# MLP down projection: the low parts of half of the ordinary weight loads are made by ScalarE and an accumulating GpSimd transfer instead of by VectorE

## The reference

```python
u = jax.nn.relu(rms_norm(h, mlp_norm_g) @ w_up)
h = h + (u * u) @ w_down
```

## Time and profile before

| | |
|---|---|
| time, median of 3 runs (lowest to highest) | 2503.59 us (2503.17 to 2504.42) |
| span of the profiled execution | 2504.0 us |
| TensorE busy | 2480.6 us (99%) |
| VectorE busy | 1753.6 us (70%) |
| ScalarE busy | 1257.8 us (50%) |
| GpSimd busy | 29.5 us (1%) |
| DMA queue of the loads | 463.53 MB, 55.2% of 16 engines |
| chain that ended last | PE 94%, issue 4%, DVE 2% |

### The profile page before, as it was taken

How to read it: one execution, slowest core, us unless ns; L and a number is a source line. 1 busy time by engine, 2 the same in 40 slices (tenths; PEclk the granted TensorE clock), 3 DMA queues, 4 the chain that set the end, 5 groups by cost and what they waited for, 6 DMA issues and landing times.

```text
span 2504.0 us, 38061 instructions
## 1 busy us (share of the span) xinstructions
PE 2480.6 (99%) x15416; PEld 2115.6 (84%) x15416; DVE 1753.6 (70%) x1978; ACT 1257.8 (50%) x1506; POOL 29.5 (1%) x26
## 2 busy tenths in 40 slices
PE   9999999999999999999999999999999999999998
PEld 7888888888888888888888888888888888888886
DVE  6656765668668677675777777775776666777777
ACT  7655344544444444445555555544654444444543
POOL 0000000000000000000000000000000000000000
PEclk9999999999999999999999999999999999999999
DMA  9454545546546546555545454556465565556553
GB/s 381 153 183 152 176 153 193 176 164 223 193 161 231 187 171 211 193 195 183 185 153 185 153 185 153 185 170 195 150 217 185 186 200 187 183 194 198 186 188 127
DMA packets 128239, 465.97 MB, mean 186 GB/s; under 512 B 14368, under 2 KB 14624, under 8 KB 127168
## 3 DMA queue, kind: packets, MB, share of 16 engines
q1 hardware_dynamic: 127920, 463.53, 55.2%
q10 hardware_dynamic: 144, 0.02, 0.0%
HBM read 461.39 MB, written 2.10 MB: 185 GB/s over the span
## 4 chain that ended last, share of the span: by engine, by line
PE 94%; issue 4%; DVE 2%; ACT 0%; DMA 0%; SPq 0%; DVEq 0%; POOL 0%; POOLq 0%
PE job L970 30%; PE job L982 16%; PE job L938 11%; PE job L940 11%; PE job L939 11%; PE job L957 2%; PE job L958 2%; PE job L959 2%; PE att L958 2%; PE att L957 2%; PE att L959 2%; PE att L1177 1%; PE att L998 0%; DVE w_low L1593 0%; PE att L1010 0%
## 5 line engine op out<-in xcount | busy, mean ns | idle before, releaser
L1274 ACT ACTIVATE w_high<-raw 128x1024 fp32r<-128x1024 f32 (+1 forms) x883 | 919.6, 1050 | 733.9 <-PE job L940 292.4
L1593 DVE TENSOR_TENSOR w_low<-raw,w_high 128x1024 fp32r<-128x1024 f32 (+1 forms) x883 | 1047.0, 1212 | 310.5 <-ACT w_high L1274 231.0
L970 PE MATMUL job<-actA,w_high 128*128 128x512 f32 x3328 | 798.3, 391 | 0.1
L970 PEld LDWEIGHTS job<-actA,w_high 128*128 128x128 f32 x3328 | 611.8, 188 | 119.9 <-issue 0.7
L982 PEld LDWEIGHTS job<-actA,w_low 128*128 128x128 f32 x3328 | 426.7, 191 | 16.2
L982 PE MATMUL job<-actA,w_low 128*128 128x256 f32 x3328 | 431.7, 283 | 0.0
L1796 DVE TENSOR_TENSOR slots<-job,slots 128x512 f32<-128x512 f32 x102 | 70.5, 691 | 344.1 <-ACT slots L1466 343.5
L938 PE MATMUL job<-w_high,actB 128*128 128x512 f32 x736 | 288.6, 392 | 2.5 <-DVE w_low L1593 2.0
L939 PE MATMUL job<-w_low,actB 128*128 128x512 f32 x736 | 287.1, 390 | 0.0
L940 PE MATMUL job<-w_high,actB 128*128 128x512 f32 x736 | 287.0, 390 | 0.0
L938 PE MATMUL job<-w_high,actA 128*128 128x512 f32 x576 | 230.9, 401 | 0.0
(11 more groups left out here) (257 smaller groups left out, 1906.0 us busy)
## 6 DMA issues: line engine op xcount, KB each, us to landing
raw<-in_weights SPq DMA_DIRECT2D x855, 512.0 KB, 4.2
M<-in_mem_t SPq DMA_DIRECT2D x8, 256.0 KB, 8.0
slots<-in_mem SPq DMA_DIRECT2D x2, 1024.0 KB, 12.2
M<-in_x_t SPq DMA_DIRECT2D x4, 512.0 KB, 13.8
H<-in_x SPq DMA_DIRECT2D x2, 1024.0 KB, 9.0
out<-H SPq DMA_DIRECT2D x8, 256.0 KB, 3.2
slots<-in_w_small SPq DMA_DIRECT2D x1, 1024.0 KB, 9.7
slots<-in_post_mix_g SPq DMA_DIRECT2D x1, 1024.0 KB, 4.3
```

Source lines behind the costliest of these rows:

```text
L970: mm = nc.tensor.matmul(J[job.buf][:, x, :], w_high[:, w % AHEAD, cols], act_both[job.act][:, c, :, :].rearrange("p a t -> p (a t)"), star ...
L1274: nc.scalar.activation(w_high[:, s % AHEAD, cols], raw[:, s % RAW_SLOTS, cols], ACT.Copy)\
L1593: nc.vector.tensor_tensor(w_low[:, s % AHEAD, cols], raw[:, s % RAW_SLOTS, cols], w_high[:, s % AHEAD, cols].bitcast(F32), ALU.subtract).t ...
```

## The change

`by_transfer(w)` picks side 1 of each "eight" pair (k1, k7, k9, k15, k17, k19), except where window w - 5 is of kind "features", which drops k1 of the first job in each block. That leaves 5 windows in each of the four first jobs and 6 in each of the three second ones: 38 windows. For these

- VectorE does nothing;
- ScalarE, right behind the high part, writes the *negated* high part into `w_low` (a second ACTIVATE from the same `raw` slot, with scale -1) and raises `neg_made`;
- GpSimd waits for `neg_made` and issues a DMA of the same 512 KB of weights out of HBM into that `w_low` slot, which adds to what stands there;
- TensorE waits for the landing of that DMA (`low_landed`, one semaphore for each of the five slots) and not for `low_ready`.

`low_ready` now counts the other windows only (`LOWS`). SP, before it reuses a raw slot, and VectorE, before `sums_of` overwrites two, wait for `neg_made` where the window was one of the 38 (`raw_wait`).

```diff
+def by_transfer(w):
+
+    job, k = WINDOW[w]
+    return (job.kind == "quads" and job.parts[k][0] == "eight" and job.parts[k][2] == 1
+            and WINDOW[w - AHEAD][0].kind != "features")
...
+        def low_wait(engine, w):
+
+            if by_transfer(w):
+                engine.wait_ge(low_landed[w % AHEAD], 16 * LANDED[w])
+            else:
+                engine.wait_ge(low_ready, LOWS[w])
+
+        def raw_wait(engine, w):
+
+            if by_transfer(w):
+                engine.wait_ge(neg_made, NEGS[w])
+            else:
+                engine.wait_ge(low_ready, LOWS[w])
...
-                    sp.wait_ge(low_ready, w - RAW_SLOTS + 1 + (part_of(w - RAW_SLOTS) == 0))
+                    raw_wait(sp, w - RAW_SLOTS + (part_of(w - RAW_SLOTS) == 0))
...
+            def split(w, s):
+
+                if by_transfer(s):
+                    pool.wait_ge(neg_made, NEGS[s])
+                    nc.gpsimd.dma_start(w_low[:, s % AHEAD, :], d["weights"][LOAD_AT[s] - 1], accum_op=ALU.add)\
+                        .then_inc(low_landed[s % AHEAD], 16)
...
             def quads(w):
                 job, k = WINDOW[w]
                 first_of(w)
-                pe.wait_ge(low_ready, w + 1)
+                low_wait(pe, w)
...
                 nc.scalar.activation(w_high[:, s % AHEAD, cols], raw[:, s % RAW_SLOTS, cols], ACT.Copy)\
                     .then_inc(high_ready, 1)
+                if by_transfer(s):
+                    nc.scalar.activation(w_low[:, s % AHEAD, :], raw[:, s % RAW_SLOTS, :], ACT.Copy, scale=-1.0)\
+                        .then_inc(neg_made, 1)
...
+                if by_transfer(s):
+                    return
                 if part_of(s) == 1:
                     sums_of(s)
                 dve.wait_ge(high_ready, s + 1)
...
-                dve.wait_ge(low_ready, s + 3 - RAW_SLOTS)
+                raw_wait(dve, s + 1 - RAW_SLOTS)
+                raw_wait(dve, s + 2 - RAW_SLOTS)
```

More of the change, by code:

```diff
@@ L508, in part_of @@
     return job.parts[k][2] if job.kind == "quads" and job.parts[k][0] == "seven" else None
+def by_transfer(w):
+    job, k = WINDOW[w]
+    return (job.kind == "quads" and job.parts[k][0] == "eight" and job.parts[k][2] == 1
+            and WINDOW[w - AHEAD][0].kind != "features")
+LOWS = list(itertools.accumulate(int(not by_transfer(w)) for w in range(PLAN.windows)))
+NEGS = list(itertools.accumulate(int(by_transfer(w)) for w in range(PLAN.windows)))
+LANDED = [sum(by_transfer(v) for v in range(w % AHEAD, w + 1, AHEAD)) for w in range(PLAN.windows)]
 SUMS = list(itertools.accumulate(int(part_of(w) == 1) for w in range(PLAN.windows)))
@@ L722, in build @@
         sums_made = sem("sums_made")
+        neg_made, low_landed = sem("neg_made"), [sem(f"low_landed{i}") for i in range(AHEAD)]
         out_ready, half_done, wide_done = sem("out_ready"), sem("half_done"), sem("wide_done")
@@ L853, in stage @@
                                             ALU.pow).then_inc(S["rstd"], 1)
-            walk(n, lambda w: None, lambda w, s: None, stage)
+            def split(w, s):
[3 more added lines that the diff above has]
+                        .then_inc(low_landed[s % AHEAD], 16)
+            walk(n, lambda w: None, split, stage)
         @block.tensor
@@ L1268, in split @@
                 if s >= AHEAD and WINDOW[s - AHEAD][0].kind == "features":
-                    act.wait_ge(low_ready, s - AHEAD + 1)
+                    act.wait_ge(low_ready, LOWS[s - AHEAD])
                     act.wait_ge(wide_done, WIDE[s - AHEAD])
```

## The result

The changed kernel takes 2577.56 us (median of 4 runs, 2575.18 to 2578.83) beside 2503.67 of the kernel before (4 runs): ratio 1.0292, interval 1.0279 to 1.0306. It is 74 us slower, where 56 were forecast.

A forecast was written before the change was run, and what follows sets the result against it. TensorE was taken as the bound, so VectorE's relief gains nothing; 44 us of landing stalls plus 12 us of lowered clock, 56 us on the profiled 2504.0, gave 2560 us, range 2512 to 2618.

The forecast's parts named there:

- What bounds it, and what is taken away: Down projection: TensorE bounds; eight VectorE stalls (5.4 us) ahead of k4 and k6 stay; 46 us off VectorE gain nothing.
- ScalarE: Quad jobs: 38 negated copies add 40 us on a half-idle engine; the delays of about 1 us stay hidden.
- Where the new stalls stand: Quad jobs: 14 waits for the landing, at k7 and k15 of seven jobs, with 2.88 or 3.81 us of room.
- The other 24 windows cost nothing: Quad jobs: k9, k17, k19 and k1 have enough room for the landing, so no stalls there.
- the prediction's own signs of being wrong: Stalls at k9 or k17, L under 3.8 us, or a loss outside the quad jobs.
- The price of a landing: Stalls at k7 and k15: 14 L - 49.6 us, with L at 6.7 us giving 44 us.
- L: Time from raised neg_made to the transfer's landing: 6.7 us, bounds 3.2 and 13.8 us.
- The clock: Behind the new stalls: half of the 14 bring 1.2 GHz, 1.7 us lost each, 12 us; bounds none and 24 us.
- in time: k7 and k15: landing at or below 3.8 us, +1 us at 3.2, time 2505 us; chance 7%.
- VectorE's stalls go too: Ahead of k4 and k6: the 5.4 us vanish and L is short, time 2498.6 us; chance 3%.
- Transfers queue: Quad jobs: DMA engines full, L 9 to 10 us, late loads, lower clock: 107 us, time 2611 us; chance 25%.
- A plain price: k7 and k15: transfer costs what a load does, 4.5 us, clock unaffected: 13 us, time 2517 us; chance 12%.

The follow-up runs named there:

- plain copy: Changed kernel, but the GpSimd transfer copies the weights over the negated high part and does not add: 2540.08 us, ratio 1.0146.
- one step further: Kernel before, no transfers, square and split of the last quarter of u 8 windows later instead of 6: 2503.57 us, ratio 0.9997.
- the u work later: Changed kernel with the square and split of the last quarter of u put 8 windows later: 2587.12 us, ratio 1.0332.
- k7 and k15 alone: Changed kernel with only k7 and k15 of each quad job done by transfer, 14 windows in place of 38: 2572.77 us, ratio 1.0275.
- negated copy first: Changed kernel, but ScalarE makes the negated copy ahead of the high part, so transfers start 0.95 us earlier: 2573.25 us, ratio 1.0278.

## Why the prediction came out as it did

*What bounds it, and what is taken away:* right. The eight old stalls are there at the same size (4.2 us idle against 4.1), all ahead of k7, and 41 us off VectorE bought nothing.

*ScalarE:* right, and shown alone at a ratio of 1.0004.

*Where the new stalls stand:* right for the 14 of k7 and k15, in place and cause. "The other 24 windows cost nothing" was nearly right in the changed kernel (three k9 of second jobs, 3.3 us), though a stall at k9 was one of the prediction's own signs of being wrong. And it was so only because the stalls in front cover the others: without those, k17 and k9 stall in every job. k9's transfer lands 8.6 to 9.5 us after its issue, far over the 6.7 that I gave to all, and k7 of second jobs, 1.5 to 1.7 us late, does not cover that.

*The price of a landing:* the step that was mis-sized. I gave one L of 6.7 us to all: 4.5 of a load, 1.5 for the second stream, 0.7 for GpSimd. In engine time the second stream was about right (2.8 us for an addition, 1.5 for a copy), and so was GpSimd's part (0.87 us). But L is not one number. From the end of the negated copy to the restart of TensorE it is 565.98 - 559.96 = 6.0 us at k7 of the first job and 587.97 - 579.53 = 8.4 at k15, since at k15 a burst of raw loads is in front of the transfer and beside it. So k7 cost less than forecast (10.6 + 4.9 idle against 15.3 + 8.7), and k15 more (29.4 against 20.2). That the errors cancel in part, 51 us with k9 and the 0.16 us each against 44, is luck.

*The clock:* the mechanism was right, half of the stalls too few. 11 of the 14 stalls of k7 and k15, where I let 7, brought the lower level: all seven k15 and all four k7 of first jobs. 20 us against 12; ten had 3.4 us at that level, as the kernel's start had shown, one 6.8. A nearer row lay in the trace of before, the one stall of 3.8 us, ahead of line 998, in the middle of steady work:

```profile
1757.56 3.50 PE L998 MATMUL att<-ident,H 128*128 128x128 f32 x16 [3.78 <-DVE H L1985]
...
1757.40:1760.80 3.40, 3.24 (x16) 3.27 (x17) 3.40 (x9) 2.09 (x6) 0.00 (x0) 0.50 0.00 0
```

The prediction compared its k15 with the 2.0 us of the start alone; this one is of k15's size and had the whole 3.4 us behind it.

*The base:* the span of a profiled execution is about 1.9 us below its time (2573.3 beside 2575.18), so the span 2504.0, to which the sum was added, is not to be compared with the median as it stands; that is 2 us and changes nothing.

*The rivals:* "in time" and "VectorE's stalls go too" are out; the shortest landing of all 38 is 5.1 us. "Transfers queue" had the right place with the wrong partner: the engines' share in the stretch rose from 0.57 to 0.68, not to full, and k7 and k15 do not wait for another transfer (alone they are as late): k7 waits for little but its own transfer, k15 for raw loads too. How much of the late landings at k17 and k19 is the transfer in front of them, no run here separates. A plain price of 4.5 us was out even for a plain copy (median 6.2; 3.4 to 3.9 at k7).

The Trainium skill's fit in "DMA: Bandwidth & Descriptors" (section on the anatomy of a GpSimd-path DMA) gives 3.2 us for these bytes. Measured are 5.1 to 10.3 for the addition, and 3.4 to 7.4 (median 6.2) for the plain copy. Where little is in front, at k7 of second jobs, the copy's 3.4 to 3.6 are near the fit; between many loads of another queue it does not hold. That page's section on queues lets an engine take turns between its queues packet by packet; the 286 packets of one queue with none of the other do not look like that, but no view shows from when on the transfer had work for the engines. "Collectives: The Full Stack" (section on the bandwidth ceiling), by which an addition needs two reads and halves the rate, agrees: 2.8 against 1.5 us.

What stays open: why nothing moves for up to 4 us after the issue, where 1.6 are the transfer's own. That the rest goes with raw loads in front is shown; whether they delay the descriptors that GpSimd writes or the reading itself, no run here tells. A transfer in the same places from SP's queue was not tried.

## What to carry to other kernels

Count the room of a window, from the moment its buffer comes free to the moment its consumer starts, and compare that with the landing under the traffic of just that moment, not with the median of the loads. Work taken from an engine that is not waited for is worth nothing, whatever its share of busy time, and a transfer in its place is a chain of a software issue, the loads in front and a second read. Where an engine stalls another a few times for a microsecond, look first at what stands ahead in its own list: moving that was worth 3.7 us here, and one step further it was worth nothing.

## What the runs showed of the hardware that was not expected

- An accumulating transfer of GpSimd into SBUF had its first packet 1.6 us after its issue with nothing else moving, and landed after 5.3. With raw loads running in front of it, no packet came for 4 us (k7 of the first job with the u work later). Issued 2.0 us earlier than in the changed kernel, it let TensorE go on 0.9 us later.
- An accumulating transfer of 512 KB takes 2.8 us of the sixteen engines, a copy 1.5, an addition of half the bytes 1.5. The median landings are 8.9, 6.2 and 6.8 us.
- Eleven stalls of 2.5 to 4.6 us, in the middle of steady work, each went with 3.4 us (once 6.8) at 1.2 GHz; in the same kernel those of 0.8 to 1.7 us did not. That cost 20 us on top of 51. The length of a stall does not settle it: over the down projection of all traces here, none of the stalls under 1.7 us brought the lower level and all 36 over 3.5 us did, but of the 56 in between only 32. One of 1.8 us did (with k7 and k15 alone), one of 2.9 us did not (negated copy first).
